# A seventh short-form quad in the later MLP pairs, and three of four residual blocks accumulated onto seeded PSUM banks

## The reference

```python
h2 = rmsnorm(x, norm2_g[l])
x = x + jnp.square(jax.nn.relu(h2 @ w_mlp_in[l])) @ w_mlp_out[l]     # 2048 -> 8192 -> 2048
...
h2 = rmsnorm_2(x, g_mlp[l])
x = x + jnp.square(jax.nn.relu(h2 @ w_up[l])) @ w_down[l]            # second block, same shape
```

## Time and profile before

| | us |
|---|---|
| median of 3 runs | 2802.53 (2802.35 to 2804.4) |
| the profiled execution | 2803.19 |
| its span in the trace | 2801.5 |
| PE busy | 2785.7 (99%) |
| DVE busy | 2225.8 (79%) |
| ACT busy | 1489.1 (53%) |

### The profile page before, as it was taken

How to read it: one execution, slowest core, us unless ns; L and a number is a source line. 1 busy time by engine, 2 the same in 40 slices (tenths; PEclk the granted TensorE clock), 3 DMA queues, 4 the chain that set the end, 5 groups by cost and what they waited for, 6 DMA issues and landing times.

```text
span 2801.5 us, 33866 instructions
## 1 busy us (share of the span) xinstructions
PE 2785.7 (99%) x13102; PEld 2302.2 (82%) x13102; DVE 2225.8 (79%) x2487; ACT 1489.1 (53%) x1674; POOL 1.6 (0%) x7
## 2 busy tenths in 40 slices
...
PEclk9999999999999999999999999999999999999999
...
GB/s 326 157 222 200 205 153 217 201 189 198 256 229 217 218 247 233 243 212 245 227 231 228 222 207 207 204 202 225 198 240 207 245 215 245 228 243 233 241 228 166
DMA packets 372640, 616.99 MB, mean 220 GB/s; under 512 B 23040, under 2 KB 96384, under 8 KB 371840
## 3 DMA queue, kind: packets, MB, share of 16 engines
...
...
## 4 chain that ended last, share of the span: by engine, by line
PE 97%; DVE 2%; issue 0%; ACT 0%; DMA 0%; SPq 0%; DVEq 0%; ACTq 0%
PE ACC L872 76%; PE TB L878 11%; PE ACC L878 7%; DVE WL L1617 1%; PE TB L993 0%; DVE XTL L2180 0%; DMA RAW<-in_w_in_dram 0%; ACT WH L1144 0%; DVE HT L2102 0%; DVE FG L1630 0%; DVE YBL L1641 0%; PE TB L1026 0%; PE TB L1029 0%; PE TB L1058 0%; PE TB L1035 0%
## 5 line engine op out<-in xcount | busy, mean ns | idle before, releaser
L1144 ACT ACTIVATE WH<-RAW 128x1024 fp32r<-128x1024 f32 (+1 forms) x1023 | 1030.1, 1020 | 1018.8 <-PE ACC L872 642.2
L1617 DVE TENSOR_TENSOR WL<-RAW,WH 128x1024 fp32r<-128x1024 f32 (+1 forms) x1023 | 1187.3, 1174 | 410.3 <-ACT WH L1144 407.3
L872 PE MATMUL ACC<-WH,XTH 128*128 128x512 f32 (+1 forms) x1692 | 658.3, 389 | 0.4 <-DVE XTL L1691 0.4
L872 PE MATMUL ACC<-WL,XTH 128*128 128x512 f32 (+1 forms) x1692 | 655.2, 387 | 0.0
L872 PE MATMUL ACC<-WH,XTL 128*128 128x512 f32 (+1 forms) x1692 | 655.1, 387 | 0.0
L872 PEld LDWEIGHTS ACC<-WH,XTH 128*128 128x128 f32 x1692 | 317.8, 188 | 67.1 <-DVE XTL L1691 0.8
L872 PEld LDWEIGHTS ACC<-WH,XTL 128*128 128x128 f32 x1692 | 317.8, 188 | 65.0
L872 PEld LDWEIGHTS ACC<-WL,XTH 128*128 128x128 f32 x1692 | 317.9, 188 | 63.7
L872 PE MATMUL ACC<-WH,YAH 128*128 128x512 f32 x864 | 336.2, 389 | 0.0
L872 PE MATMUL ACC<-WL,YAH 128*128 128x512 f32 x864 | 336.1, 389 | 0.0
L872 PE MATMUL ACC<-WH,YAL 128*128 128x512 f32 x864 | 336.1, 389 | 0.0
...
## 6 DMA issues: line engine op xcount, KB each, us to landing
...
RAW<-in_w_mlp_out_dram SPq DMA_DIRECT2D x128, 512.0 KB, 5.2
RAW<-in_w_down_dram SPq DMA_DIRECT2D x128, 512.0 KB, 5.1
...
```

The source lines that it names most:

```text
L872: ins = e.matmul(ACC[:, 2 * (b % 2) + half, 0:n], p[:, k, xs], q[:, t, 0:n], start=(k == 0 and m == 0), stop=(k == nk - 1 and m == 2))
L1144: e.activation(WH[u % NSPL][:, ts, 0:n], RAW[u % NRAW][:, ts, 0:n], ACT.Copy).then_inc(hi, 1)
L1617: e.tensor_tensor(l, r, h, ALU.subtract).then_inc(lo, 1)
```

## The change

- `SEVEN_I` gets row index 4: seven of eight quads of the pairs j = 2 to 7 are in short form. Quad 7 alone stays direct. The buffers for the seventh quad's sums are the `T` set again. The activation sums have seven forms instead of six. Some move to other tiles: the fifth sum is made in FG, and its rounded and low parts lie in three pieces, in XTH/XTL and in new fp32r views over JK and over unused constants (`JKR`, `CSTR`).
- For the output blocks c = 1, 2, 3 (all but the very last block), X is copied by ACT into the ACC banks before the block (`residual_seed`), PE accumulates onto it (no `start`), and ACT copies the banks back to X (`residual_out`). DVE keeps the residual of c = 0 and of the last block. The step for c = 0, 1, 2 stands one unit later than before (for j < 7), that of c = 3 at the same unit.
- `x_sums` makes the sums of both parts for the quads 0 to 3 at once and earlier, and every step after it stands one unit earlier. In `hidden_out` the square is a step of its own, behind the next cut.

```diff
-    SEVEN_I = (0, 1, 2, 3, 5, 6)
+    SEVEN_I = (0, 1, 2, 3, 4, 5, 6)
-    SETS = ("T", "Y", "H", "T", "Y", "H")
+    SETS = ("T", "Y", "H", "T", "Y", "H", "T")
+    SEEDED = {}
+    for tag in "12":
+        for j in range(8):
+            for c in (1, 2, 3):
+                if (tag, j, c) != ("2", 7, 3):
+                    SEEDED[B["o" + tag, j, c]] = len(SEEDED) + 1
...
-        at(("xs", tag), f + 2)
+        at(("xs", tag), f + 1, 2)
         at(("rsb", tag), f + 3)
-        at(("xs", tag), f + 4, 6)
-        at(("xs_hi", tag), f + 10, 2)
-        at(("xs", tag), f + 12, 3)
+        at(("xs", tag), f + 4, 5)
+        at(("xs_hi", tag), f + 9, 2)
+        at(("xs", tag), f + 11, 3)
...
-                    at(("ev", "h" + tag), last("h" + tag, 0, b))
+                    at(("ev", "h" + tag), last("h" + tag, 0, b) + 1 - b, 2)
...
             for c in range(4):
-                at(("ev", "o" + tag), last("o" + tag, j, c))
+                at(("ev", "o" + tag), last("o" + tag, j, c) + (j < 7 and c < 3))
+                b = B["o" + tag, j, c]
+                if b in SEEDED:
+                    at(("seed", tag), UE[b - 2] + (2 if c > 1 else 1 - (c == 0)))
...
-                                   start=(k == 0 and m == 0), stop=(k == nk - 1 and m == 2))
+                                   start=(k == 0 and m == 0 and b not in SEEDED), stop=(k == nk - 1 and m == 2),
+                                   skip_group_check=b in SEEDED)
...
-            if i == 0 and b >= 2:
+            if i == 0 and b in SEEDED:
+                e.wait_ge(seeded, SEEDED[b])
+            elif i == 0 and b >= 2:
                 e.wait_ge(acc[b % 2], b // 2)
...
+        def residual_seed(tag):
+            for j in range(8):
+                for c in range(4):
+                    b = B["o" + tag, j, c]
+                    if b not in SEEDED:
+                        continue
+                    e.wait_ge(acc[b % 2], b // 2)
+                    evicted(e, *(("o" + tag, j - 1, c) if j else ("wo" + tag, c)))
+                    e.activation(ACC[:, 2 * (b % 2):2 * (b % 2) + 2, :], X[:, :, 512 * c:512 * c + 512], ACT.Copy).then_inc(seeded, 1)
+                    yield
+
+        def residual_out(tag):
+            for j in range(8):
+                for c in range(4):
+                    b = B["o" + tag, j, c]
+                    if b in SEEDED:
+                        multiplied(e, "o" + tag, j, c)
+                        e.activation(X[:, :, 512 * c:512 * c + 512], ACC[:, 2 * (b % 2):2 * (b % 2) + 2, :], ACT.Copy
+                                     ).then_inc(acc[b % 2], 1)
+                    yield
...
-                    residual(("o" + tag, j, c), c)
+                    if B["o" + tag, j, c] not in SEEDED:
+                        residual(("o" + tag, j, c), c)
                     yield
```

More of the change, by code:

```diff
@@ L221, in build @@
     xs, xs_hi, xs_lo, diag, rsb = sem("x_sums"), sem("x_sums_hi"), sem("x_sums_lo"), sem("root_diagonal"), sem("root_rows")
+    seeded = sem("residual_seeded")
     t_sum, t_hi, t_lo = sem("weight_sums"), sem("weight_sums_hi"), sem("weight_sums_lo")
@@ L243, in build @@
     YAH, YAL = sb("YAH", [P, 8, L], F32R), sb("YAL", [P, 8, L], F32R)
+    over = ExitStack()
+    CSTR = sb("CSTR", [P, 5 * P], F32R, to=over)
+    over.close()
     CST = sb("CST", [P, 5 * P])
@@ L250, in build @@
     PR = GBP[:, :, :].rearrange("p a n -> p (a n)")[:, 0:768].rearrange("p (k j) -> p k j", j=32)
+    over = ExitStack()
+    JKR = sb("JKR", [P, 512], F32R, to=over)
+    over.close()
     JK = sb("JK", [P, 512])
@@ L394, in build @@
     m2.close()
-    AX = XTF[:, 1024:1024 + 512 * NI].rearrange("p (s k r t) -> p s k r t", s=NI, k=2, r=2)
+    AX = XTF[:, 512:512 + 512 * NI].rearrange("p (s k r t) -> p s k r t", s=NI, k=2, r=2)
     FGS = {"1": FG, "2": FG2}
     SX = {tag: f[:, 0:512 * NI].rearrange("p (f s t) -> p f s t", f=4, s=NI) for tag, f in YF.items()}
-    SX4 = {tag: f[:, 3072:3072 + P * NI].rearrange("p (s t) -> p s t", s=NI) for tag, f in YF.items()}
+    SX4 = {tag: f[:, 0:P * NI].rearrange("p (s t) -> p s t", s=NI) for tag, f in FGS.items()}
     TR = {tag: f[:, :].rearrange("p (f n) -> p f n", f=4) for tag, f in FGS.items()}
@@ L404, in build @@
     SXR = [x[:, 0:512 * NI].rearrange("p (f s t) -> p f s t", f=4, s=NI) for x in (XTHF, XTLF)]
-    S4R = [x[:, 3072:3072 + P * NI].rearrange("p (s t) -> p s t", s=NI) for x in (XTHF, XTLF)]
+    S4_PARTS = (slice(0, 4), slice(4, 6), slice(6, 7))
+    S4R = [[y.rearrange("p (s t) -> p s t", t=P) for y in (x[:, 3584:4096], JKR[:, 2 * P * k:2 * P * k + 2 * P], CSTR[:, (3 + k) * P:(4 + k) * P])]
+           for k, x in enumerate((XTHF, XTLF))]
     XSTEPS = NI + 7
@@ L903, in sums @@
             def sums(f):
-                return [y[:, f, rec.form, :] for y in SXR] if f != S_4 else [y[:, rec.form, :] for y in S4R]
+                if f != S_4:
+                    return [y[:, f, rec.form, :] for y in SXR]
+                part, k = [(p, rec.form - c.start) for p, c in enumerate(S4_PARTS) if c.start <= rec.form < c.stop][0]
+                return [y[part][:, k, :] for y in S4R]
             def weight_sums(f):
@@ L1463, in sums_split @@
             yield
-            e.activation(S4R[0], SX4[tag], ACT.Copy).then_inc(xs_hi, 1)
+            for part, forms in enumerate(S4_PARTS):
+                ins = e.activation(S4R[0][part], SX4[tag][:, forms, :], ACT.Copy)
+            ins.then_inc(xs_hi, 1)
             yield
+        def residual_seed(tag):
[16 more added lines that the diff above has]
+                                     ).then_inc(acc[b % 2], 1)
+                    yield
         def x2_squares():
@@ L1574, in _ @@
                  ("xs_hi", "1"): lambda: sums_split("1"), ("xs_hi", "2"): lambda: sums_split("2"),
-                 ("sq", "y"): y_squares,
+                 ("sq", "y"): y_squares, ("ev", "o1"): lambda: residual_out("1"), ("ev", "o2"): lambda: residual_out("2"),
+                 ("seed", "1"): lambda: residual_seed("1"), ("seed", "2"): lambda: residual_seed("2"),
                  "block1_end": block1_end, ("ev", "za"): za_out, "ua_put": lambda: put("ua", UA[:, :, 30:30 + L], ua_put),
@@ L2145, in x_sums, with both_parts @@
             r, x3, m, sx, sx4 = {"1": R_1, "2": R_4}[tag], {"1": "x1", "2": "x3"}[tag], XSTEPS * (int(tag) - 1), SX[tag], SX4[tag]
+            def both_parts(quads):
+                for n, i in quads:
+                    xh, xl = (x[:, 2 * i:2 * i + 2, :].rearrange("p k (r t) -> p k r t", r=2) for x in XB[tag])
+                    e.tensor_tensor(AX[:, n], xh, xl, ALU.add).then_inc(xs, 1)
+            multiplied(e, "wo" + tag, 3)
+            e.wait_ge(turned, TN["m" + tag, 3] + 1)
+            e.wait_ge(turn_lo, 2 * TN[x3, 1] + 2)
+            both_parts([(n, i) for n, i in enumerate(SEVEN_I) if i < 4])
+            yield
             e.wait_ge(rooted, rooted_at(r))
```

11 lines of the change are left out of this document (3 added, 8 removed).

## The result

| us | before | changed |
|---|---|---|
| median | 2802.51 (4 runs, 2802.35 to 2804.4) | 2843.69 (4 runs, 2843.06 to 2846.02) |
| span of the profiled execution | 2801.5 | 2841.3 |

The changed kernel is slower: ratio 1.0146, 95% interval 1.0134 to 1.0158, or +41.2 us. The forecast was 2835, the range 2818 to 2850. In the changed kernel line 898 is before's 878 (`products`), 891 before's 872, 1667 before's 1617 (cut), 1680 to 1684 before's 1630 to 1634 (weight sums), 1691 before's 1641 (their low parts), 1169 before's 1144 (ACT's cut).

The account below looks back on a forecast made before the run. PE was taken to bound the kernel, with DVE falling behind in the pairs after the change. The span of 2801.5 - 8.2 + 43 + 0 - 2.2 = 2834.1 us, with the median's 1.0, gave 2835 us, range 2818 to 2850.

Parts of the forecast that it names:

- What bounds the kernel: Whole kernel before the change: PE, busy in 99% of the span at 2.4 GHz, sets the time by matmuls times 0.2267 us.
- item 1: PE's path in the pairs: 3 matmuls fewer for each of 12 new short quads, -8.2 us.
- Item 2: Quads 3 to 6 of a pair: each costs DVE 6.72 us and PE 4.76, so DVE's lead falls 1.96 each.
- Item 3: Start of each of 12 pairs: ACT's copy of block c = 3 delays DVE's cut; with restart 3.58 each, +43 us.
- Item 4: Output stretches and other places: ACT's new seeds and copies make PE wait nowhere, 0 us.
- Item 5: Start of pair j = 1 in both MLPs: later square and earlier activation sums shorten waits, -2.2 us (-4 to +2).
- The mean: Rival for the pairs: DVE works far enough ahead on average, so the kernel gets faster, 2792 us; chance 0.10.
- The offload: Rival at the pair's start: work moved to ACT lets DVE cut earlier, no change, some 2803 us; chance 0.06.
- The worse rival: Output stretches: a new ACT instruction precedes the tight cut in each of 14, +11 us, 2846, or 2857; chance 0.15.
- The rows foretold: Profile after: 36 fewer matmuls, about 24 PE waits for cuts of 1.5 and 1.8 us at quads 5 and 6.

## Why the prediction was right, point by point

- **What bounds the kernel; item 1.** Right: 36 matmuls less, an unchanged clock, and time lost only where PE waits for DVE's cuts.
- **Item 2, the rate.** Right, and shown twice: the steps are 6.72, 6.72 and 6.72, and taking 0.66 from each gives 34.5 us back, 31.0 of them in the twelve pairs. Six quads instead of seven give all of it back.
- **Item 3, the copy in ACT's queue.** Right: copy at T0 + 0.20 (I had 0.26), DVE's cut at T0 + 2.21 (2.30). Its trade is shown by the kernel with c = 3 on DVE, 9.0 us faster. The two waits came out as 1.30 and 1.65 where I had 1.5 and 1.8. Part of that is only how the view counts: with 0.28 added to each a pair loses 3.5, I had 3.58. For the twelve pairs I had 43 and the trace has 42.4.
- **Item 4, seeds and copies elsewhere.** Right but for one place: none of PE's waits is for `seeded`, and the seeds and copies come at 1.02 us each, but in the last output stretch a copy holds the cuts and costs 0.9 where I had 0. That wait of 0.60 is in every kernel here with seeded blocks, and in neither of the two without (the kernel before, and the one with nothing moved). I treated the relief of c = 1 and 2 as worthless ("they relieve nobody whom PE waits for"). With seven quads and the residual of c = 2 one unit later it is worth 9.5 us (nothing moved against c = 3 alone on DVE). The starting time in my layout came from the kernel before, with all residuals on DVE and that of c = 2 a unit earlier, and whether the relief counts beside that order is open. With six quads it is worth nothing.
- **Item 5, the start of pair j = 1.** The step that failed, by its sign: I had -2.2, at most +2, and it was +3.9 (+4.6 at the MLPs' starts, -0.7 in pair j = 1). I had looked at the wait for the activation sums, and it did go. But the sums that come a unit earlier take ACT's queue with them: the rounding stands there, waits 3.45 us for DVE, and the cut behind it is late. It takes the seventh form too: with six, in the same early place, PE does not wait. The rounding one unit later gave 5.2 us back. The square gained little (0.7 us is all that pair j = 1 gave back in both MLPs), since it still stands in front of the cut of unit 3, and DVE cuts units 2 and 3 together before it goes on; moving it further changed nothing.
- **The sum.** I had -8.2 + 43 - 2.2 = +32.6 for the span; the trace has +39.8, of which -8.2, +42.4, +3.9 and +0.9 are placed and 0.8 are not. Of the 7.2 between them, item 5 is 6.1 and item 4 is 0.9. The median stands 2.4 above the span of the profiled execution, where I had 1.0 from before, which makes up the rest of the 8.7 by which 2835 fell short.
- **The rivals.** The mean (DVE 77.8 of 85.8 us busy) was no guide. The offload does help DVE's mean, 52 us less with six quads, without any effect on the time; and what helped at the one tight place was the opposite, work given back to DVE. The rule of the Trainium skill that I weighed there ("Perfetto Trace Analysis", section "Optimizing Scalar/DVE Operations": with a saturated DVE, moving work to ScalarE may make sense) held for c = 1 and 2 at their later places, and was reversed for c = 3 by what stood behind the moved instruction. The two effects cancel: with all three blocks moved 2843.69, with none 2844.15. The worse rival (a new instruction of ACT in front of the cut in every output stretch) came true in the last stretch alone, for 0.9 us. It is not what made the difference.
- **The rows foretold** came as written: about 24 new waits, DVE without idle time behind T0 + 2.2. The exceptions are pair j = 1, where PE waits 2.13 and not 0.7, and the period: PE has 82.9 of 85.8 us there. I had taken the window of 78 us for the period, which is 1117.82 - 1034.86 = 82.96 us in the kernel before. The sum did not use it.
